# The opening of a transformer block: modulation in seven chunks, scale and shift side by side, five pieces of w_mod on TensorE, the turn of x interleaved

## Time and profile before

| | us |
|---|---|
| runs of the kernel before | 2694.97, 2696.22, 2697.15 (median 2696.22) |
| span of the profiled execution | 2694.1 |
| PE busy | 2626.5 (97%) |
| DVE busy | 2076.6 (77%) |
| ACT busy | 1158.2 (43%) |
| DMA, mean | 180 GB/s |

### The profile page before, as it was taken

The page is one execution under the profiler, slowest core; times in us unless marked ns, Lnnn a source line. Parts: engine busy times, 40 slices in busy tenths (PEclk is TensorE's granted clock), DMA queues, the critical chain, the costliest instruction groups (busy, mean ns, idle before and its releaser), DMA issues.

```text
span 2694.1 us, 40797 instructions
## 1 busy us (share of the span) xinstructions
PE 2626.5 (97%) x14114; PEld 2205.6 (82%) x14114; DVE 2076.6 (77%) x3029; ACT 1158.2 (43%) x1553; POOL 210.8 (8%) x334
## 2 busy tenths in 40 slices
PE   5999999999999999999999999999999999999998
PEld 4788888888788888887878888888888887888886
DVE  7956666666766666626657999999999998888988
ACT  4344444444622222223254444444444444454454
POOL 0030000000000000002300111111111111111000
PEclk8999999999999999999999999999999999999999
DMA  9942322332277777736843665656656565888894
GB/s 362 338 113 85 86 80 84 87 87 83 67 224 219 219 217 216 219 97 222 278 157 93 164 164 134 159 141 151 149 140 159 130 164 197 322 301 304 309 322 171
DMA packets 477847, 485.64 MB, mean 180 GB/s; under 512 B 24603, under 2 KB 381234, under 8 KB 475040
## 3 DMA queue, kind: packets, MB, share of 16 engines
q1 hardware_dynamic: 442160, 384.87, 47.3%
q0 software_dynamic: 25664, 94.93, 11.7%
q10 hardware_dynamic: 9904, 4.26, 0.6%
HBM read 428.28 MB, written 34.75 MB: 172 GB/s over the span
## 4 chain that ended last, share of the span: by engine, by line
PE 90%; DVE 5%; ACT 2%; issue 2%; DMA 1%; SPq 1%; DVEq 0%; POOL 0%; ACTq 0%; POOLq 0%
PE acc_bank L849 15%; PE acc_bank L851 14%; PE acc_bank L850 14%; PE acc_bank L1280 8%; PE acc_bank L1284 4%; PE bank_ta L1280 3%; PE bank_pb L1280 3%; PE bank_tb L1280 3%; PE two_banks L1280 3%; PE two_banks L849 2%; PE two_banks L850 2%; PE two_banks L851 2%; PE bank_tb L1284 1%; PE bank_ta L1284 1%; PE bank_pb L1284 1%
## 5 line engine op out<-in xcount | busy, mean ns | idle before, releaser
L840 DVE TENSOR_TENSOR w_lo<-raw,w_hi 128x1024 fp32r<-128x1024 f32 x215 | 262.9, 1223 | 369.1 <-ACT w_hi L834 369.0
L834 ACT CAST w_hi<-raw 128x1024 fp32r<-128x1024 f32 x215 | 225.4, 1049 | 541.5 <-PE acc_bank L851 375.4
L849 PE MATMUL acc_bank<-h_hi,w_hi 128*128 128x512 f32 x1124 | 447.3, 398 | 8.1 <-DVE h_lo L2007 8.1
L851 PE MATMUL acc_bank<-h_hi,w_lo 128*128 128x512 f32 x1124 | 439.1, 391 | 0.0
L850 PE MATMUL acc_bank<-h_lo,w_hi 128*128 128x512 f32 x1124 | 438.6, 390 | 0.0
L849 PEld LDWEIGHTS acc_bank<-h_hi,w_hi 128*128 128x128 f32 x1124 | 211.6, 188 | 52.0 <-issue 8.1
L851 PEld LDWEIGHTS acc_bank<-h_hi,w_lo 128*128 128x128 f32 x1124 | 211.4, 188 | 45.3
L850 PEld LDWEIGHTS acc_bank<-h_lo,w_hi 128*128 128x128 f32 x1124 | 211.8, 188 | 41.9
L1280 PE MATMUL acc_bank<-h_pair,s_hi 128*128 128x512 f32 x640 | 160.3, 392 | 0.0
L1993 DVE SCALAR_TENSOR_TENSOR acc<-raw,csil,acc 128x512 f32<-128x512 f32 x180 | 135.0, 750 | 12.3 <-DMA raw<-in_w_mod_dram 8.0
L1280 PEld LDWEIGHTS acc_bank<-h_pair,s_hi 128*128 128x128 f32 x640 | 115.1, 189 | 20.6
(11 more groups left out here) (730 smaller groups left out, 6346.8 us busy)
## 6 DMA issues: line engine op xcount, KB each, us to landing
raw<-in_w_in_dram SPq DMA_DIRECT2D x148, 512.0 KB, 3.9
raw<-in_w_mod_dram SPq DMA_DIRECT2D x96, 512.0 KB, 4.5
raw<-in_w_ffn_up_dram SPq DMA_DIRECT2D x92, 512.0 KB, 5.0
raw<-in_w_ffn_down_dram SPq DMA_DIRECT2D x86, 512.0 KB, 5.9
raw_odd<-in_w_ffn_up_dram SPq DMA_DIRECT2D x80, 512.0 KB, 5.1
raw_more<-in_w_ffn_down_dram SPq DMA_DIRECT2D x63, 512.0 KB, 6.2
mods_low<-in_w_mod_dram SPq DMA_DIRECT2D x32, 512.0 KB, 10.0
raw<-in_w_out_dram SPq DMA_DIRECT2D x32, 512.0 KB, 4.5
```

Source lines behind the costliest of these rows:

```text
L834: act.copy(w_pair(g, gp)[0][:], raw[n % RAW][:]).then_inc(hi_ready, 1)
L840: dve.tensor_tensor(w_l[:], raw[n % RAW][:], w_h[:].bitcast(F32), ALU.subtract).then_inc(lo_ready, 1)
L849: pe.matmul(o, stat[0], mov[0], start=start, stop=False)
L851: return pe.matmul(o, stat[1], mov[0], start=False, stop=stop)
```

## The change

Scale and shift of the same kts are now made together: a w_mod piece has 256 columns of scale and the same 256 of shift for two kts, in two DMAs of 1 KB rows (chunks of two kts), or 512 and 512 columns for one kt (the one chunk of four kts, fifth of seven). One product on DVE covers scale and shift: 512 elements, or 1024 in chunk 4, in 102 products. Five of the 64 pieces (DIRECT) are not multiplied on DVE: PE multiplies their 128x128 blocks with a column of silu(c), in the same accumulation as the chunk's sums. The rows of x are loaded with two w_mod pieces between them. The turn of x on PE is cut into five parts, with the sums of chunks 0 and 1 and piece kv 0 in between; ACT's copies of it have modulate(0) to (3) in between. Matmuls wait for the h of their own kt, not of the whole piece, and three pieces are cut in two on PE. The order of the pieces is new; kv 7 comes fourth from the end. q's second half uses bank SC1, the v turns use A[2] and PB and stand between f and g. Three small copies of vectors move from DVE to ACT, the first part of the lower bounds' work on DVE to behind the last h_low. The gain sums in the later loop (`gain_sum`, `take_gain`) do what mod_sum and take_cols did there.

```diff
-MODS_HEAD = 64
+CHUNKS = (2, 2, 2, 2, 4, 2, 2)
+FIRST_KT = [sum(CHUNKS[:n]) for n in range(len(CHUNKS))]
+CHUNK_PIECES = [16 if n == 4 else 8 for n in CHUNKS]
+FIRST_PIECE = [sum(CHUNK_PIECES[:n]) for n in range(len(CHUNKS))]
+DIRECT = {1: (4,), 2: (2, 5), 3: (2, 5)}
+CHUNK_OPS = [16 - 2 * len(DIRECT.get(n, ())) for n in range(len(CHUNKS))]
+OPS_DONE = [sum(CHUNK_OPS[:n + 1]) for n in range(len(CHUNKS))]
+SUMS_HEAD = len(CHUNKS)
+MODS_HEAD = OPS_DONE[-1] // 2
...
+START_PIECES = [("kv", 0), ("kv", 1), ("iq", 0), ("kv", 2), ("iq", 1), ("q", 0), ("kv", 3), ("f", 0), ("g", 0),
+                ("kv", 4), ("kv", 5), ("iq", 2), ("kv", 6), ("iq", 3), ("kv", 7), ("q", 1), ("f", 1), ("g", 1)]
+KV0, KV1, IQ0, KV2, IQ1, Q0, KV3, F0, G0, KV4, KV5, IQ2, KV6, IQ3, KV7, Q1, F1, G1 = range(START)
+LOAD_AFTER = {(0, 5): KV0, (2, 1): KV1, (2, 6): IQ0, (3, 1): KV2, (3, 6): IQ1, (4, 0): Q0, (4, 2): KV3, (4, 5): F0,
+              (4, 8): G0, (4, 11): KV4, (4, 14): KV5, (5, 2): IQ2, (5, 5): KV6, (6, 0): IQ3, (6, 3): KV7, (6, 5): Q1}
+SPLIT_AFTER = {(0, 15): KV0, (2, 8): KV1, (3, 2): IQ0, (3, 9): KV2, (4, 0): IQ1, (4, 2): Q0, (4, 5): KV3, (4, 8): F0,
+               (4, 11): G0, (4, 14): KV4, (5, 2): KV5, (5, 7): IQ2, (5, 13): KV6, (6, 4): IQ3, (6, 9): KV7, (6, 13): Q1}
+COLUMNS_AFTER = {1: 1, 2: 4, 3: 3, 4: 3, 5: 5, 6: 3}
+LOW_AFTER = {1: (3, 5), 2: (7, 9), 3: (6, 8), 4: (4, 6), 5: (8, 10, 12, 14), 6: (6, 8)}
...
+        def chunk_cols(ch, v):
+            lo = 8 * (ch % 2) + 4 * v
+            return SC0[:, lo:lo + CHUNKS[ch]]
+
+        def mod_place(ch, i):
+            slot = (FIRST_PIECE[ch] + i) % MODS_IN
+            if ch == SUMS_HEAD - 1 and slot < TT:
+                return xT[:, 2 * slot:2 * slot + 2, :]
+            return MODS_SLOTS[slot]
...
+        def mod_tiles(ch):
+            per = 4 // CHUNKS[ch]
+            return [(i, k, i * per + k) for i in range(CHUNK_PIECES[ch]) if i not in DIRECT.get(ch, ()) for k in range(per)]
...
+            def load_mod(ch, i):
+
+                j = FIRST_PIECE[ch] + i
                 if j >= MODS_IN:
-                    sp.wait_ge(mod_ops, 2 * (j - MODS_IN) + 2)
-                sp.dma_start(MODS_SLOTS[j % MODS_IN], w_mod_t[:, 2 * i:2 * i + 2, col:col + 512]).then_inc(mod_landed[j % MODS_IN], 16)
-                if j in LOAD_AFTER:
-                    load_start(LOAD_AFTER[j])
+                    old = max(n for n in range(len(CHUNKS)) if FIRST_PIECE[n] <= j - MODS_IN)
+                    sp.wait_ge(*mod_used(old, j - MODS_IN - FIRST_PIECE[old]))
+                if ch == SUMS_HEAD - 1 and i == 0:
+                    sp.wait_ge(hx_ready, 8)
+                per = 4 // CHUNKS[ch]
+                for v, first in enumerate((MOD_SC1, MOD_SH1)):
+                    col = (first + FIRST_KT[ch]) * P
+                    sp.dma_start(mod_slot(ch, i, v), w_mod_t[:, per * i:per * i + per, col:col + CHUNKS[ch] * P]
+                                 ).then_inc(mod_landed[j % MODS_IN], 16)
+                if (ch, i) in LOAD_AFTER:
+                    load_start(LOAD_AFTER[ch, i])
+
+            load_x(0)
+            load_x(1)
+            load_mod(0, 0)
+            load_x(2)
+            load_mod(0, 1)
+            load_x(3)
...
+            def chunk_sums(ch):
+
+                if ch >= 2:
+                    pe.wait_ge(mod_taken, ch - 1)
+                first = True
+                for i in DIRECT.get(ch, ()):
+                    mod_arrived(pe, ch, i)
+                    for k in range(2):
+                        for v in range(2):
+                            for n in range(CHUNKS[ch]):
+                                t = pe.matmul(chunk_cols(ch, v)[:, n:n + 1], mod_slot(ch, i, v)[:, k, n * P:n * P + P],
+                                              csil[:, 2 * i + k:2 * i + k + 1], start=first, stop=False)
+                                first = False
+                    t.then_inc(direct_done, 1)
+                pe.wait_ge(mod_ops, OPS_DONE[ch])
+                for v in range(2):
+                    for n in range(CHUNKS[ch]):
+                        lo = (v * CHUNKS[ch] + n) * P
+                        for h, src in enumerate(mod_sums(ch)):
+                            t = pe.matmul(chunk_cols(ch, v)[:, n:n + 1], src[:, lo:lo + P], ones[:, 0:1], start=first, stop=(v, n, h) == (1, CHUNKS[ch] - 1, 1))
+                            first = False
+                t.then_inc(mod_summed, 1)
...
+            pe.wait_ge(xn_ready, TT)
+            turn_x(0, 4)
+            chunk_sums(0)
+            turn_x(4, 8)
+            kv_piece(KV0)
+            turn_x(8, 10)
+            chunk_sums(1)
+            turn_x(10, KT)
+            kv_piece(KV1)
+            chunk_sums(2)
+            iq_piece(IQ0, 0, 4)
+            kv_piece(KV2)
+            chunk_sums(3)
+            iq_piece(IQ1, 0, 4)
+            half_piece(Q0, 0, 8)
+            kv_piece(KV3)
+            half_piece(F0, 0, 8)
+            half_piece(G0, 0, 4)
+            chunk_sums(4)
+            half_piece(G0, 4, 8)
+            kv_piece(KV4)
+            kv_piece(KV5)
+            chunk_sums(5)
+            iq_piece(IQ2, 0, 4)
+            kv_piece(KV6)
+            iq_piece(IQ3, 0, 2)
+            chunk_sums(6)
+            half_piece(Q1, 0, 6)
+            iq_piece(IQ3, 2, 4)
+            kv_piece(KV7)
+            half_piece(Q1, 6, 8)
+            half_piece(F1, 0, 8)
+            pe.wait_ge(kv_out, 4)
+            for i in range(TT):
+                for b in range(2):
+                    t = pe.transpose(v_turn(i)[:, b * P:(b + 1) * P], kvT[:, 2 + b, i * P:(i + 1) * P], ident[:])
+            t.then_inc(v_turned, 1)
+            half_piece(G1, 0, 8)
...
+            def take_x(lo, hi):
+                for kb in range(lo, hi):
+                    act.wait_ge(x_turned, kb + 1)
+                    act.copy(xT[:, kb, :], TURN_BANKS[kb % 2]).then_inc(xT_ready, 1)
+
+            act.wait_ge(vec_turned, 2)
+            for j, rows in ((1, 72 + FB), (2, 2 * FB), (3, FB)):
+                t = act.copy(vec[:, j, 0:rows], SC1[:, j * P:j * P + rows])
+            t.then_inc(vec_ready, 1)
+            split_start(KV0)
+            take_x(0, 5)
+            act.wait_ge(cols_ready, 1)
+            act.wait_ge(xT_ready, 1)
+            modulate(0)
+            take_x(5, 6)
+            act.wait_ge(xT_ready, 2)
+            modulate(1)
+            take_x(6, 11)
+            act.wait_ge(cols_ready, 2)
+            act.wait_ge(xT_ready, 3)
+            modulate(2)
+            take_x(11, 12)
+            act.wait_ge(xT_ready, 4)
+            modulate(3)
+            take_x(12, KT)
             act.wait_ge(xT_ready, KT)
-            split_start(2)
-            modulate_chunk(0)
-            split_start(3, 4, 5, 6)
-            modulate_chunk(1)
-            split_start(7)
-            take_partial(0, 4)
-            split_start(8, 9)
+            split_start(KV1, IQ0)
             modulate_chunk(2)
-            split_start(10)
-            take_partial(1, 7)
-            split_start(11, 12)
-            take_partial(2, 9)
-            split_start(13)
+            split_start(KV2, IQ1, Q0)
             modulate_chunk(3)
-            split_start(14, 15, 16)
-            act.wait_ge(multiplied, 14)
+            split_start(KV3)
+            take_partial(0, Q0)
+            split_start(F0, G0)
+            take_partial(1, F0)
+            split_start(KV4, KV5, IQ2)
+            modulate_chunk(4)
+            take_partial(2, G0)
+            split_start(KV6, IQ3)
+            modulate_chunk(5)
+            split_start(KV7, Q1)
+            modulate_chunk(6)
+            split_start(F1)
+            act.wait_ge(multiplied, IQ3 + 1)
+            act.copy(iraw[:], TA[:]).then_inc(E["i_ready"], 1)
+            act.copy(qh[:], TB[:]).then_inc(E["q_ready"], 1)
+            act.wait_ge(multiplied, KV7 + 1)
             for b in range(4):
                 act.copy(kvT[:, b, :], KV_BANKS[b][:]).then_inc(kv_out, 1)
-            split_start(17)
-            act.wait_ge(multiplied, 15)
-            act.copy(iraw[:], TA[:]).then_inc(E["i_ready"], 1)
-            act.copy(qh[:], TB[:]).then_inc(E["q_ready"], 1)
+            split_start(G1)
...
+            def mod_product(ch, n):
+
+                i, k, kt = mod_tiles(ch)[n]
+                w = mod_place(ch, i).rearrange("p v (k n) -> p k v n", n=CHUNKS[ch] * P)[:, k]
+                dst = mod_sums(ch)[n % 2].rearrange("p (v n) -> p v n", v=2)
+                if k == 0:
+                    mod_arrived(dve, ch, i)
+                if n < 2:
+                    if ch >= 2:
+                        dve.wait_ge(mod_summed, ch - 1)
                     return TS(dst, w, csil[:, kt:kt + 1], None, ALU.mult).then_inc(mod_ops, 1)
-                dve.wait_ge(mod_ops, 2 * j + half - 1)
+                dve.wait_ge(mod_ops, OPS_DONE[ch] - CHUNK_OPS[ch] + n - 1)
                 return STT(dst, w, csil[:, kt:kt + 1], dst, ALU.mult, ALU.add).then_inc(mod_ops, 1)
...
```

(69 more changed lines are left out.)

163 lines of the change are left out of this document (72 added, 91 removed), and 3 rows, old and new, of the table START_PIECES.

## The result

| | before | after |
|---|---|---|
| median of the runs, us | 2696.22 (2694.97 to 2697.15) | 2719.72 (2717.86 to 2721.36) |
| span of the profiled execution, us | 2694.1 | 2718.1 |
| granted clock, mean | 0.993 | 0.988 |

The kernel became slower: ratio 1.0088, interval 1.0077 to 1.0099. The time forecast was 2703, with 2690 to 2711 as its range; the result lies outside it. The direction was right, the size was not: 6.7 us were forecast and 23.5 came.

What follows compares the result with a forecast made beforehand. PE in the opening bounds the kernel; 0.65 start + 8.5 direct - 15.3 idle - 4.4 slow clock + 14.1 idle + 3.2 at the head = 6.75, so 2696.2 + 6.7 = 2702.9, say 2703; range 2690 to 2711.

Steps and rivals of the forecast that it cites:

- Bound and place: PE is busy behind the opening, so the first scores' start, 175.1 us, moves the kernel's end one for one.
- Start: x3 loads behind two w_mod pieces, so the first turn of x on PE comes at 24.2, 0.65 us later.
- Direct products on PE: Five direct pieces add 40 one-column matmuls to PE in the opening, 8.5 us.
- Idle time: PE's waits at hand-overs in the opening: 14.1 us, and 3.2 before the first scores, for 15.3 before.
- The clock: The 4.4 us that matmuls lost at 1.2 GHz after long idle in the opening go; no new falls counted.
- rival 3: Light stretches and gaps in the opening throw PE's clock, 2.2 us a fall; three give 2709.5; chance 0.18.
- DMA: w_mod loads in 1 KB rows, near 350 GB/s, cost 7 us in all but leave the sum alone.
- Head: Hand-over to the first head: 16.5 us from KV7's end to scores, 13.3 covered, so PE waits 3.2.
- Rivals 1 and 2: No idle gap on PE, 2689, chance 0.17; half the gaps (7 us) real, no change, 2696, chance 0.19.
- rival 1: No idle gap on PE in the opening: scores at 167.7, 7.4 us faster, 2689; chance 0.17.

Runs made afterwards that it cites:

- e1: The kernel after without its five direct pieces, so that DVE multiplies all 64: 2705.39 us, ratio to before 1.0035.
- e4: The kernel before with the sums of vector pieces 4, 5 and 6 made three times, 48 more one-column matmuls in long rows: 2716.14 us.
- e5: The kernel before with 48 more one-column matmuls, one behind each group of three heavy ones in six pieces: 2708.03 us.
- e2b: The kernel after with the direct pieces of chunks 2 and 3 moved ahead of KV1 and KV2: 2708.10 us.
- e6: e1 with gaps covered by order: KV1, KV2, IQ1 split earlier, Q0 within IQ1, KV7 before IQ3's second half, POOL's tables earlier: 2691.38 us.
- e3: The kernel after with POOL's tables and prob's memset ahead of its wait for k and v: 2719.76 us.

## Why the prediction was wrong, step by step

- **Bound and place.** Right in the main. Behind the scores PE is not busy without a break, as the prediction had read from one stretch of 40 us: from 176 us in before and 200 us in after it is idle 30 and 26 us of 2518. But that part kept its length to 0.6 us, so one moment, 175.1, was the right thing to forecast. The 0.6 is partly luck: over the nine traces the part lies between 2518.0 and 2523.8 us.
- **Start.** 0.65 forecast, 0.39 measured.
- **Direct products on PE.** 8.5 forecast; e1 takes 8.3 away with them. Right. Of the 10.0 us of added work the other 1.7 are in e1 too. The new order has more joints between turns, sums and pieces, and I had carried over the 1.6 us of the old one; that the joints are the 1.7 is not shown.
- **Idle time.** 14.1 + 3.2 = 17.3 forecast, 15.8 measured. By gap, forecast against trace: turns 0.7, 1.35 and 1.0 against one of 0.7; KV1 2.8 against 3.0; KV2 1.3 against 1.9; IQ1 3.1 against 4.6 in two; F0 to G0 0.6 against 0.9; sums(4) 0.6 against 0.3; KV4 2.7 against 0.5; kcur 3.2 against 3.85. The walk through the written orders found most places; the total is partly luck, for 2.4 us too much at the turns and 2.2 at KV4 stand against 3.3 too little elsewhere. At KV4 the clock itself hid the wait: a fall from 135.5 to 138.9 stretched the half of G0 ahead of it from 2.8 to 4.3 us.
- **The clock: the step that failed.** The prediction took 4.4 us off for the old falls and put nothing in their place; rival 3 said "sums seem to count little" and "I count none". The falls cost 17.6. Forecast was -4.4 for this term, measured +12.5 between the two kernels (17.6 against 5.1): 16.9 us, the whole of the miss of 16.7 (23.4 against 6.7). All other terms came to 11.2 in the forecast (6.75 + 4.4) and to 10.9 in the trace, as 1.5 us less of idle time and 1.5 more of work cancel. The two rows I had the earlier trace rows showed falls near idle time, and the other light rows of that kernel, sums of 1.7 us, brought none; I read from them that light work doesn't count. The change made rows of 5.1 us, longer than any in that trace, and e4 against e5 shows that such rows bring a fall where PE has no idle time. Rival 3 named the mechanism and its price (2.2 a fall; seven periods before the scores' wait give 17.6, 2.5 each), but counted three falls. The light rows and gaps at the seven are the sums and direct pieces of chunks 1, 2, 3 and the sums of chunk 4, and the gaps at KV1, KV2 and IQ1: all that rival 3 lists but the gap at KV4, which hardly came, and KV2's besides; an eighth begins in the wait for kcur. The list was to be counted in full, not as three.
- **The price of many short gaps.** In after a fall comes behind a short gap or a light row, on heavy work at 0.43 instead of 0.23; before, half of the 20.5 us at half the clock (10.3) lay in the 8.1 and 5.6 us of idle time, where it costs nothing; after, only 4.0 of 39.1. That cutting one long gap into several short ones raises its price is read from these two traces; no run tried it by itself.
- **DMA.** The sum was left alone, and that holds as far as e1 tests it. Chunk rows of 1 KB moved 351 GB/s in the first turns (23 to 41 us), the 350 estimated. The wait of SP for slots that PE frees was not in the prediction at all; its cost stays open between 0 and the 4.7 us of e2b; in e1, where that wait is gone, the idle time stayed.
- **Head.** 16.5 us from KV7's end to the scores forecast, 17.1 measured.
- **Rivals 1 and 2** (no gaps, half the gaps) did not come. e6 shows the way to rival 1: with 5.5 us of gaps the time is 2691.

## What to carry to other kernels

When work with few moving columns is put on a full TensorE, price it by its length in a row and by what stands behind it: forty one-column matmuls cost 8.3 us themselves and 7.2 more in clock, and 48 of them between heavy matmuls cost 8.7 us of clock less than the same 48 in three rows. A light row can be paid twice where heavy work follows, and so, it seems, can a gap, so fill it with heavy work that is ready (another piece's first kts), rather than make it shorter on the other engine. And read the clock's cost from "how much of the lower level fell on work", not from its mean: 0.93 in the kernel before meant a loss of 5.1 us, 0.92 in e1 one of 10.4.

## What the runs showed of the hardware

The granted clock fell to 0.5 while PE was busy for the whole of a stretch (92 to 104 us of e4), in a row of one-column matmuls; the same matmuls one by one between heavy ones left it at 1.00 there (e5). The fall begins inside the long rows (in e4 at 96.0, the row at 92.25). In the nine traces there are nine rows of 5.1 us, and each has a fall, of 6.8 us in eight of them and 10.2 in one (e3). Of the twelve rows of 3.4 us each has one too, of 3.4 us in nine and 6.8 in three (chunk 1 in after and e3, chunk 4 in e6). Rows of 1.7 us mostly have none, but not always: besides the one in e5, falls of 3.4 us follow chunk 1's sums in e1 (a wait of 0.4 us ahead of them), chunk 3's in e6 (a wait of 0.9 ahead) and chunk 0's in e6, among the turns with no such wait:

```profile
30.50:32.50 2.00, 1.99 (x17) 2.00 (x18) 1.89 (x4) 0.56 (x1) 0.00 (x0) 1.00 1.11 349
32.50:36.50 4.00, 4.00 (x23) 4.00 (x23) 2.15 (x6) 2.37 (x5) 0.00 (x0) 0.57 1.11 349
```

In the other traces that row has no fall, so a short row's fall can't be foretold from the order alone. The runs compare one moving column with 512; what lies between is open. At the lower level the heavy matmuls take 0.427 us each instead of 0.228, and a one-column matmul (two records) takes 0.43 instead of 0.22 too, so light work also doubles. The Trainium skill (TensorE: Matmul & The Clock Gate, HAM oscillation) puts such falls down to gaps in which TensorE is idle. The falls behind KV1's gap (3.0 us) and KV2's (1.9) agree with that in kind, though the section speaks of longer ones; the rows of e4 show that gaps aren't needed.
